# Relative bias of the banded attention: added to the scores by VectorE instead of by products on TensorE

## The reference, cut to what matters

```python
scores = jnp.einsum('bnqhd,bnkhd->bnhqk', qc, k_band).astype(jnp.float32) * (Dh ** -0.5)
dist = jnp.arange(CHUNK)[:, None] + LEFT_CHUNKS * CHUNK - jnp.arange(BAND)[None, :]
rel_idx = jnp.clip(dist, -MAX_REL, MAX_REL) + MAX_REL
bias = rel_table[:, rel_idx].astype(jnp.float32)
...
scores = jnp.where(valid[None, :, None, None, :], scores + bias[None, None], NEG_INF)
p = jax.nn.softmax(scores, axis=-1).astype(v.dtype)
```

## Time and profile before

| | |
|---|---|
| median of 3 runs | 2302.64 us |
| profiled execution, own time | 2303.89 us |
| its span, first to last instruction | 2302.2 us |
| TensorE busy | 2235.0 us, 97% |
| TensorE weight loads | 1848.3 us, 80% |
| VectorE busy | 1275.7 us, 55% |
| ScalarE busy | 1119.2 us, 49% |
| GpSimd busy | 124.8 us, 5% |
| DMA | 399.22 MB, mean 173 GB/s |
| mean granted TensorE clock | 0.990 |

### The profile page before, as it was taken

One profiled execution on the slowest core, in us unless ns is written; L12 is line 12 of the kernel. 1 busy time (PEld: TensorE's weight loads), 2 busy tenths in 40 slices (PEclk: granted clock), 3 DMA queues, 4 the chain that ended last, 5 costly groups with the idle time before them and its releaser, 6 DMA issues.

```text
span 2302.2 us, 32811 instructions
## 1 busy us (share of the span) xinstructions
PE 2235.0 (97%) x12407; PEld 1848.3 (80%) x12407; DVE 1275.7 (55%) x1457; ACT 1119.2 (49%) x1505; POOL 124.8 (5%) x172
## 2 busy tenths in 40 slices
PE   7999999999999999999999999999999999999995
PEld 6788888888888778878888878887887788778884
DVE  4445456464545647484755554466545845556455
ACT  6445445454445647383745454444443544444433
POOL 5000000000000101001010000000000200000002
PEclk9999999999999999999999999999999999999998
DMA  6765655656566545353545755645557466445552
GB/s 218 223 214 169 194 175 164 205 182 202 192 183 183 147 125 151 104 173 111 164 129 179 246 172 176 197 133 152 158 184 265 134 226 189 133 145 164 184 192 101
DMA packets 213991, 399.22 MB, mean 173 GB/s; under 512 B 21048, under 2 KB 37555, under 8 KB 212960
## 3 DMA queue, kind: packets, MB, share of 16 engines
q1 hardware_dynamic: 205664, 365.61, 51.7%
q0 software_dynamic: 5616, 21.23, 2.8%
q10 hardware_dynamic: 2576, 10.49, 1.3%
HBM read 388.82 MB, written 8.45 MB: 173 GB/s over the span
## 4 chain that ended last, share of the span: by engine, by line
PE 87%; ACT 4%; issue 3%; DVE 3%; DMA 2%; POOL 1%; DVEq 0%; SPq 0%; ACTq 0%; POOLq 0%
PE stream_psum L548 25%; PE stream_psum L550 25%; PE stream_psum L549 25%; PE heads_psum L714 3%; PE heads_psum L526 3%; ACT w_high L967 1%; PE heads_psum L891 1%; ACT work L967 1%; DMA w_raw<-in_w_mem_kv 1%; DMA w_raw<-in_w_in 1%; PE heads_psum L854 1%; PE heads_psum L833 1%; ACT L967 1%; DVE work L1549 1%; PE heads_psum L722 1%
## 5 line engine op out<-in xcount | busy, mean ns | idle before, releaser
L1383 DVE TENSOR_TENSOR w_low<-w_raw,w_high 128x1024 fp32r<-128x1024 f32 (+1 forms) x700 | 836.2, 1211 | 756.4 <-ACT w_high L967 754.8
L967 ACT ACTIVATE w_high<-w_raw 128x1024 fp32r<-128x1024 f32 (+1 forms) x700 | 715.4, 1047 | 479.9 <-PE stream_psum L550 395.0
L548 PE MATMUL stream_psum<-w_high,x_high 128*128 128x512 f32 x1856 | 744.8, 401 | 6.7 <-ACT proj L967 3.0
L550 PE MATMUL stream_psum<-w_high,x_low 128*128 128x512 f32 x1856 | 725.4, 391 | 0.0
L549 PE MATMUL stream_psum<-w_low,x_high 128*128 128x512 f32 x1856 | 725.0, 391 | 0.0
L548 PEld LDWEIGHTS stream_psum<-w_high,x_high 128*128 128x128 f32 x1856 | 349.9, 189 | 82.6 <-issue 6.3
L550 PEld LDWEIGHTS stream_psum<-w_high,x_low 128*128 128x128 f32 x1856 | 349.5, 188 | 74.6
L549 PEld LDWEIGHTS stream_psum<-w_low,x_high 128*128 128x128 f32 x1856 | 350.1, 189 | 69.4 <-issue 1.9
L548 PE MATMUL stream_psum<-w_high,y_high 128*128 128x512 f32 x896 | 355.6, 397 | 10.0 <-DVE w_low L1383 7.9
L550 PE MATMUL stream_psum<-w_high,y_low 128*128 128x512 f32 x896 | 350.1, 391 | 0.0
L549 PE MATMUL stream_psum<-w_low,y_high 128*128 128x512 f32 x896 | 349.9, 391 | 0.0
(11 more groups left out here) (276 smaller groups left out, 1290.1 us busy)
## 6 DMA issues: line engine op xcount, KB each, us to landing
w_raw<-in_w_in SPq DMA_DIRECT2D x528, 512.0 KB, 4.5
w_raw<-in_w_out SPq DMA_DIRECT2D x128, 512.0 KB, 4.8
w_raw<-in_w_mem_kv SPq DMA_DIRECT2D x32, 512.0 KB, 5.0
work<-rows_scratch POOLq DMA_DIRECT2D x8, 512.0 KB, 6.2
proj<-in_mem SPq DMA_DIRECT2D x2, 1024.0 KB, 7.9
residual<-in_x ACTq DMA_DIRECT2D x1, 2048.0 KB, 12.7
mkv_scratch<-proj POOLq DMA_DIRECT2D x4, 512.0 KB, 4.5
mem_high_scratch<-y_high POOLq DMA_DIRECT2D x4, 512.0 KB, 4.0
```

The source lines that it names most:

```text
L548: pe.matmul(acc, hi[:, k, sl(m)], w, start=first, stop=False)
L550: last = pe.matmul(acc, lo[:, k, sl(m)], w, start=False, stop=final)
L967: return act.activation(dst, src, func, **kw)
L1383: tt(WL[:, c % RING, 0:width], RAW[:, c % RING, 0:width], WH[:, c % RING, 0:width].bitcast(F32), ALU.subtract).then_inc(lo_done, 1)
```

## The change: what it does

The scores of the banded attention are left in PSUM without bias. VectorE adds the band to them and writes the sum to the work area where the exponentials are to stand (L1669 of the new kernel); the maxima are taken from there, and the exponentials are computed in place. The products with `flip` and the matrix itself are gone, with GpSimd's two instructions that made it. For the band to lie in row order, row p has to start at place 127 - p of the table. The table is therefore stored in device memory 128 times over for each head, and loaded with a step of 383 values from row to row. The masked quarter moves from partitions 64 to 127 to partitions 0 to 63.

```diff
-    rel_d = nc.dram_tensor("rel_scratch", (A_H, BIASW), F32, kind="Internal").ap()
+    rel_d = nc.dram_tensor("rel_scratch", (A_H, P, BIASW), F32, kind="Internal").ap()
...
-        flip = sb("flip", [P, P])
...
-        AT_V = {k: steps_of(sem(f"{k}_dve"), ["k", "g", "max0", "max1", "neg", "pt", "rs", "f", "fg"]) for k in "am"}
+        AT_V = {k: steps_of(sem(f"{k}_dve"), ["k", "g"] + (["bias"] if k == "a" else []) + ["max0", "max1", "neg", "pt", "rs", "f", "fg"]) for k in "am"}
...
-            c(pool.memset(flip[:], 0.0))
-            c(pool.affine_select(out=flip[:], in_=flip[:], compare_op=ALU.not_equal, fill=1.0, base=1 - P,
-                                 pattern=[[1, P]], channel_multiplier=1))
...
-                pool.dma_start(rel_d, wk(6.5, BIASW)[0:8, :]).then_inc(rel_st, 16)
+                pool.dma_start(rel_d, over(wk(6.5, BIASW)[0:8, :], P)).then_inc(rel_st, 16)
...
-                               bass.AP(rel_d.tensor, 0, [[1, P], [BIASW, A_H], [1, S]])).then_inc(rel_bw, 16)
+                               bass.AP(rel_d.tensor, P - 1, [[BIASW - 1, P], [P * BIASW, A_H], [1, S]])).then_inc(rel_bw, 16)
...
-                if not full:
-                    pe.wait_ge(rel_m, rel_need)
...
-                        last = pe.matmul(H[:, h, a:b], qT[...], kT[...], start=True, stop=full)
-                        if not full:
-                            last = pe.matmul(H[:, h, a:b], flip[:], wk(9, 3 * U)[:, (h0 + h) * BIASW + a:(h0 + h) * BIASW + b], start=False, stop=True)
+                        last = pe.matmul(H[:, h, a:b], qT[...], kT[...], start=True, stop=True)
...
-                        last = f(wk(2, 4 * w)[:, h * w + a:h * w + b], H[:, h, a:b], ACT.Exp, bias=ST[:, 24 + 2 * h + m:25 + 2 * h + m],
+                        e = wk(2, 4 * w)[:, h * w + a:h * w + b]
+                        last = f(e, H[:, h, a:b] if full else e, ACT.Exp, bias=ST[:, 24 + 2 * h + m:25 + 2 * h + m],
...
+                if not full:
+                    src = wk(2, 4 * w).rearrange("p (h n) -> p h n", h=4)
+                    dve.wait_ge(rel_m, rel_need)
+                    bw = wk(9, 3 * U).rearrange("p (h n) -> p h n", h=A_H)[:, h0:h0 + 4, :]
+                    tt(src, H[:, :, 0:w], bw, ALU.add).then_inc(*signal(AT_V[kind], "bias"))
+                    dve.wait_ge(*done(AT_V[kind], "bias", n))
...
-                dve.memset(BW[64:P, :, 64:P], NEG).then_inc(rel_m, 1)
-                dve.memset(BW[64:P, :, BIASW - 64:BIASW], NEG).then_inc(rel_m, 1)
+                dve.memset(BW[0:64, :, 64:P], NEG).then_inc(rel_m, 1)
+                dve.memset(BW[0:64, :, BIASW - 64:BIASW], NEG).then_inc(rel_m, 1)
```

More of the change, by code:

```diff
@@ L238, in load_count @@
             return n * 4 + (16 * (c // RING) + 16 + extra)
-        N_CONSTS = 9 + 3 * (7 + 2 * 6) + 2
+        N_CONSTS = 7 + 3 * (7 + 2 * 6) + 2
         FEATURES = ((YH, YL), (XH, XL))
@@ L802, in dn, with attend @@
                 yield from outputs(DN_PE, done(DN_V, "fg", g), wk(10).rearrange("p (m n) -> p m n", m=M), 2)
-            def attend(kind, q, n, evac_need, h0=0, rel_need=None):
+            def attend(kind, q, n, evac_need):
                 steps, act, dve = AT_PE[kind], AT_ACT[kind], AT_V[kind]
@@ L832, in attend @@
                     for m, a, b in ((0, 0, n0), (1, n0, n0 + S)):
-                        last = pe.matmul(H[:, h, a:b], qT[:, h * S + m * P:h * S + (m + 1) * P], kT[:, h * S:h * S + b - a], start=True, stop=full)
-                        if not full:
-                            last = pe.matmul(H[:, h, a:b], flip[:], wk(9, 3 * U)[:, (h0 + h) * BIASW + a:(h0 + h) * BIASW + b], start=False, stop=True)
+                        last = pe.matmul(H[:, h, a:b], qT[:, h * S + m * P:h * S + (m + 1) * P], kT[:, h * S:h * S + b - a], start=True, stop=True)
                 last.then_inc(*signal(steps, "scores"))
@@ L956, in _ @@
                 stream(n + L_A0, e + 6, 4, IH, IL, gla(l, q + 1, 2 * (e + 6)), first_need=e + 6)
-                stream(n + L_A1, e + 10, 4, IH, IL, attend("a", q + 2, 2 * l, 2 * (e + 10), 0, l * 3 + 3))
+                stream(n + L_A1, e + 10, 4, IH, IL, attend("a", q + 2, 2 * l, 2 * (e + 10)))
                 pe.wait_ge(out_lo, NCH + (4 * q + 12))
-                stream(n + L_Y1, e + 14, 4, OH, OL, attend("a", q + 3, 2 * l + 1, 2 * (e + 14), 4, l * 3 + 3), tiles=Y1_TILES)
+                stream(n + L_Y1, e + 14, 4, OH, OL, attend("a", q + 3, 2 * l + 1, 2 * (e + 14)), tiles=Y1_TILES)
                 pe.wait_ge(out_lo, NCH + (4 * q + 16))
@@ L1654, in dn, with attend @@
                 yield from outputs(DN_PE, g, g + 4, g * 4, lambda j: 32, 2)
-            def attend(kind, q, n, zslot, kt):
+            def attend(kind, q, n, zslot, kt, h0=0, rel_need=None):
                 steps, act_s = AT_PE[kind], AT_ACT[kind]
@@ L1854, in _ @@
                 dve.wait_ge(rel_m, l * 3 + 1)
-                dve.memset(BW[64:P, :, 64:P], NEG).then_inc(rel_m, 1)
-                dve.memset(BW[64:P, :, BIASW - 64:BIASW], NEG).then_inc(rel_m, 1)
-                stream(n + L_A1, 4, attend("a", q + 2, 2 * l, 3, 0))
+                dve.memset(BW[0:64, :, 64:P], NEG).then_inc(rel_m, 1)
+                dve.memset(BW[0:64, :, BIASW - 64:BIASW], NEG).then_inc(rel_m, 1)
+                stream(n + L_A1, 4, attend("a", q + 2, 2 * l, 3, 0, 0, l * 3 + 3))
                 def take1(b, m, acc):
@@ L1867, in take2 @@
                     dve.bn_stats(BN[:, m, b, :], r).then_inc(*signal(LN_V, f"st{m}{b}"))
-                stream(n + L_Y1, 4, attend("a", q + 3, 2 * l + 1, 3, 4), take=take1, per=len(Y1_TILES))
+                stream(n + L_Y1, 4, attend("a", q + 3, 2 * l + 1, 3, 4, 4, l * 3 + 3), take=take1, per=len(Y1_TILES))
                 stream(n + L_Y2, 4, none(), take=take2, per=len(Y2_TILES), ahead=None if l else CH * NBLK, following=AHEAD if l else LEAD)
```

## The result

The changed kernel takes 2319.33 us, the median of 4 runs (2317.28 to 2322.10), against 2303.14 us before: a ratio of 1.0069 with an interval of 1.0055 to 1.0084. It is slower by 16.2 us, where I had forecast 10.56 us faster. Its profiled execution took 2319.78 us, with a span of 2318.1 us.

What follows compares the result with a forecast made beforehand. TensorE was taken to set the end at the banded attention. From the median, 2302.64 - 10.56 = 2292.1 us, with nothing added for sum, exponentials or store; 8-in-10 range 2289.5 to 2298 us.

Steps and rivals of the forecast that it cites:

- Products removed: TensorE, banded attention: dropping 32 products with `flip` saves 2.64 us in each of 4 calls, 10.56 us.
- The sum on VectorE: Banded attention: adding the band takes 1.76 us, 1.86 us with the wait, costed at nothing.
- the margin of the exponentials: Banded attention: exponentials still end before TensorE's transposes need them, the lead shrinking from 2.59 to 0.73 us.
- The store's duration: Table store to device memory, 1.57 MB from 8 partitions: 10 us, with bounds of 4 and 61 us.
- What the weights get beside it: Weight loads during the store, 1405 to 1450: crowding costs zero, at most 4.1 us a layer.
- Turns, one for one: DMA engines carrying the store: each alternates a 1.5 KB store piece with a 2 KB weight piece, passing 2.1 MB of weights.
- The slack: Weight loads beside the store: landing in 4.8 us, they may be late by about 9.5 us before TensorE stands.
- The store starves the weights: Rival, chance 0.07: a 61 us store on half the DMA engines costs 14.7 us a layer, 2321.5 us.
- Its decision point: Weight loads beside the store: a store starts to cost TensorE time from about 46 us on.
- The store crowds the weights: Rival, chance 0.12: weight loads beside the store cost 2 to 4.1 us a layer, 2296 to 2300.3 us.
- The exponentials come late: Rival, chance 0.14: in banded attention TensorE waits 0.8 us a call, 3.2 us in all, 2295.3 us.
- the gain is not there: Rival, chance 0.05: saved time is waited for again at 1744 to 1761, or products filled a pause; 2302 us.

Runs made afterwards that it cites:

- the complete kernel without the crowding: Changed kernel with the table loaded to 128 partitions and stored from all with 8 copies each; 2292.99 us, repeated 2293.59 us, ratios 0.9953 and 0.9959.
- runs 9 and 10: Kernel before plus an unread second 1.5 MB store from partitions 0 to 7, in pieces of 512 and 3072 bytes: 2343.12 us and 2329.97 us.
- Runs 7 and 8: Kernel before plus an unread second store from partitions 0 to 7, with 64 and with 96 copies: 2301.97 us and 2317.15 us.
- runs 6 and 8: Kernel before plus an unread second store: 1.5 MB from partitions two apart, 2302.02 us; 96 copies from partitions 0 to 7, 2317.15 us.

## Why the prediction was wrong

The step that failed is the price, put at nothing, of what the store takes from the weight loads: "I take zero, with 4.1 us a layer as the upper end for ordinary crowding." It measured 14.4 and 15.7 us a layer. Term by term:

*Products removed: right.* 10.56 us were forecast; the trace has 4 x 2.62 = 10.5 us, and the complete kernel without the crowding gains 9.3 us (2302.93 to 2293.59) and 10.5 us (2303.48 to 2292.99).

*The sum on VectorE: right.* 1.76 us was forecast and 1.76 us measured; the margin of the exponentials is 0.52 us where I had 0.73, since each exponential from the work area is a little longer. No wait came of it.

*The store's duration: wrong.* This is the first step on the way to the zero: "By size from the load back, the nearest row, 1.5 x 6.7 = 10 us. I take 10 us." It took 34 to 36 us. The row was near in bytes, but went into 128 partitions; the store comes out of 8. The experiments give, for one size, 36, 19, 13 and 8 us as the partitions are neighbours, two apart, four apart, and all. My bounds of 4 to 61 us held it; the value inside them was chosen by size where the partitions decided, and among equal numbers of them their places. A store of 34 us alone would not have changed my forecast, though, since I let it last 46 us before it costs.

The Trainium skill had this number in my own text: by "SBUF — State Buffer", section "Door 1: The DMA port swizzle", partitions 0 to 7 reach two of 16 ports of 27 GB/s, an estimate of 29 us; 0, 2, ... 14 reach four, and 0, 4, ... 28 reach eight. The runs agree in the order, and for two ports nearly in the rate: 1.58 MB in 34 us is 46 GB/s. From issue to landing it is 81 GB/s for four ports (1.57 MB in 19.4 us) and 122 GB/s for eight (12.9 us), below four and eight times 27. I named the rule and gave it no weight in the price.

*What the weights get beside it: wrong, and this decided the sign.* The zero was read from two rows, and the earlier trace rows, and the first was misread. I had written "TensorE has no wait there" of the load of 1 MB at 1363. It has one, right behind (one of the five of the earlier trace rows):

```profile
1376.19 0.50 PE L548 MATMUL stream_psum<-w_high,y_high 128*128 128x512 f32 x1 [1.42 <-DVE w_low L1383]
```

The weights issued at 1364.88 landed at 1375.1, and TensorE stood for 1.42 us. So a transfer of two thirds of the size already had a rest of TensorE behind it.

The only sum that I made for a slow store was that of the rival, with "2.1 MB of weights pass these engines meanwhile, and 4.2 MB, 8 chunks, in all", and from it "It decides from a store of about 46 us on". In fact 2.03 MB passed in 33 us in all, and in the store's own 8 shares only the first of the four loads issued beside it had got through by its end, 0.26 MB, where I had 2.1 MB. Two things were wrong in it. Turns, one for one, are refuted (runs 9 and 10, and the arrivals). And I let the undisturbed half of the engines work ahead without limit, while a chunk counts only when both halves are there and only four may be under way: the first of the four loads issued beside the store, at 1413.71, was not usable until 1441.00, although its other half was there at 1417.7.

*The slack: nearly right.* I had 14.3 us from issue to landing before TensorE stands (4.8 + 9.5). TensorE ran out at 1433.64, 19.9 us after the load's issue at 1413.71; less some 2.4 us for the two conversions that is 17.5 us; products of the memory attention stand in between. The measured landing, 27.3 us after the issue, leaves 27.3 + 2.4 - 19.9 = 9.8 us of rest, which is the 9.73 measured read in another way and no test. Runs 7 and 8 are one: they put the limit between 15.7 and 22.0 us. By the 29 us estimated from the Trainium skill's page (the same section) and a load that lands when the store does (1409.5 + 29 = 1438.5, 24.8 us after its issue) the sum would have given 7.3 us of rest a layer, 14.6 us in both. That is 2306.7 us, the right sign but less than the 0.2% that I called tellable. It takes the 19.9 us and the landing with the store from the traces, which I did not have.

*The clock: left out.* The price of a wait was 4.1 us in the earlier trace rows, 1.7 of it slow products. Here 3.9 and 3.3 us follow rests of 9.7 and 10.5 us. My forecast had no term for it.

*The rivals.* "The store starves the weights" named the place, the half of the engines and the sign, with a chance of 0.07. Its number, 2321.5 us against 2319.33 measured, is near by luck: it comes from a store of 61 us and from one-for-one turns, and the store took 34 to 36 us and the turns are refuted. Its decision point was 46 us; runs 6 and 8 put it between 20.6 and 26.4 us. For the same reason the sentence that with 29 us this rival "costs nothing" was wrong: a store of 26 us cost 7 us a layer. "The store crowds the weights" had the place and the direction, but at most 4.1 us a layer. "The exponentials come late" and "the gain is not there" did not occur.

## What to carry to other kernels

A broadcast store from few partitions is small in bytes and long in time: price it by how many partitions feed it and where they lie, and spread the source before multiplying it. Its own consumers may have 88 us of room and it may still cost 15 us a layer, because a load that has a share on its DMA engines lands late with that share, here with the store's end; compare its duration with the slack from issue to use of the stream beside it. When two bounds lie 15 times apart, ask in which property the nearest row differs from the operation (here partitions, not bytes) before its value is taken.

## What the runs showed of the hardware that I had not expected

Issuing a weight load kept SyncE busy for up to 3.75 us beside the store (min/median/max in ns, 1405 to 1450 of the changed kernel), in place of 0.54 us, and 5.3 us in run 9:

```profile
L299 SPq DMA_DIRECT2D w_raw<-in_w_in x9: 539/540/3750, 1404.6 to 1448.1; - x9
```

Stores in pieces of 512 bytes from 8 neighbouring partitions took 40 us, in pieces of 3072 bytes 34 us, for the same bytes.

Of each of the four loads issued beside the store of the changed kernel's first layer, 8 of 16 arrivals came 3.4 to 7.2 us after the issue, and the other 8 only when the store was done there, 18 to 29 us after it.
